# One block for output projection and feed-forward in place of two, with the second token block's difference T2 on VectorE

## The reference, cut to what matters

```python
def swiglu(x, w_gate_up, w_down):
    gate, up = jnp.split(x @ w_gate_up, 2, axis=-1)
    return (jax.nn.silu(gate) * up) @ w_down
...
    for l in range(DEPTH):
        if l < N_A_LAYERS:
            q, k, v, lf = fox_project(rms_norm(h, g_attn[l]), w_a_in[l], b_a_f[l])
            h = h + merge_heads(fox_attention_prompt(q, k, v, lf)) @ w_a_out[l]
        else:
            j = l - N_A_LAYERS
            if j == 0:
                kb_p, vb_p = shared_kv(h, g_kv, w_kv)
            q = split_heads(rms_norm(h, g_attn[l]) @ w_b_q[j])
            h = h + merge_heads(band_attention_prompt(q, kb_p, vb_p, rel_bias[j])) @ w_b_out[j]
        h = h + swiglu(rms_norm(h, g_ffn[l]), w_gate_up[l], w_down[l])
    y_prompt = rms_norm(h, g_final)
```

## Time and profile before

| | |
|---|---|
| median of three runs | 3222.82 us (3222.11 to 3222.87) |
| profiled execution | 3220.69 us, its span 3219.0 us |
| mean granted TensorE clock | 0.959 of full speed |
| busy TensorE | 2958.0 us, 92% |
| busy VectorE | 1535.7 us, 48% |
| busy ScalarE | 1094.9 us, 34% |
| busy Pool | 948.5 us, 29% |

### The profile page before, as it was taken

The page is one execution under the profiler, slowest core; times in us unless marked ns, Lnnn a source line. Parts: engine busy times, 40 slices in busy tenths (PEclk is TensorE's granted clock), DMA queues, the critical chain, the costliest instruction groups (busy, mean ns, idle before and its releaser), DMA issues. The chain is left out here.

```text
span 3219.0 us, 47355 instructions
## 1 busy us (share of the span) xinstructions
PE 2958.0 (92%) x17916; PEld 2666.7 (83%) x17916; DVE 1535.7 (48%) x2790; ACT 1094.9 (34%) x2284; POOL 948.5 (29%) x1174
## 2 busy tenths in 40 slices
PE   8999799978599999899999997997968999998998
PEld 6777688867599999788878886886758999997887
DVE  3223188862755555433332222886645555553333
ACT  4223277721422222221133232776133222222112
POOL 1000288840544545200000001433334544540001
PEclk9999899989799999999999998998978999999999
DMA  4799577654422222432127985886331222215222
GB/s 149 176 219 244 174 259 246 212 159 136 160 63 83 71 73 83 149 112 77 49 79 197 250 203 203 261 267 176 95 105 42 83 66 79 83 49 203 85 74 84
DMA packets 479633, 448.93 MB, mean 139 GB/s; under 512 B 44160, under 2 KB 402592, under 8 KB 475184
## 3 DMA queue, kind: packets, MB, share of 16 engines
q1 hardware_dynamic: 479408, 445.91, 46.3%
HBM read 293.77 MB, written 165.81 MB: 143 GB/s over the span
## 5 line engine op out<-in xcount | busy, mean ns | idle before, releaser
L295 PE MATMUL ffn_bank<-ffn_x,ffn_w 128*128 128x256 f32 (+1 forms) x2464 | 732.0, 297 | 32.5 <-DVE ffn_x L1950 11.0
L296 PE MATMUL ffn_bank<-ffn_x,ffn_w 128*128 128x256 f32 (+1 forms) x2464 | 730.5, 296 | 0.0
L297 PE MATMUL ffn_bank<-ffn_x,ffn_w 128*128 128x256 f32 (+1 forms) x2464 | 729.0, 296 | 0.0
L295 PEld LDWEIGHTS ffn_bank<-ffn_x,ffn_w 128*128 128x128 f32 x2464 | 468.8, 190 | 36.0 <-issue 20.1
L296 PEld LDWEIGHTS ffn_bank<-ffn_x,ffn_w 128*128 128x128 f32 x2464 | 468.8, 190 | 0.0
L297 PEld LDWEIGHTS ffn_bank<-ffn_x,ffn_w 128*128 128x128 f32 x2464 | 467.7, 190 | 0.0
L295 PE MATMUL ffn_bank<-ffn_wd,ffn_hid 128*128 128x512 f32 x792 | 310.7, 392 | 28.7 <-DVE ffn_wd L1994 26.1
L296 PE MATMUL ffn_bank<-ffn_wd,ffn_hid 128*128 128x512 f32 x792 | 310.0, 391 | 0.0
L297 PE MATMUL ffn_bank<-ffn_wd,ffn_hid 128*128 128x512 f32 x792 | 310.0, 391 | 0.0
L2007 DVE TENSOR_TENSOR all_h<-ffn_bank,all_h 128x1024 f32<-128x1024 f32 x72 | 88.1, 1224 | 342.0 <-PE ffn_bank L297 342.0
L295 PEld LDWEIGHTS ffn_bank<-ffn_wd,ffn_hid 128*128 128x128 f32 x792 | 150.0, 189 | 61.2 <-issue 26.5
(11 more groups left out here) (269 smaller groups left out, 6288.2 us busy)
## 6 DMA issues: line engine op xcount, KB each, us to landing
ffn_raw<-in_w_gate_up SPq DMA_DIRECT2D x88, 512.0 KB, 5.5
ffn_draw<-in_w_down SPq DMA_DIRECT2D x44, 512.0 KB, 4.8
fox_ks<-k_split SPq DMA_DIRECT2D x16, 1088.0 KB, 5.1
band_ks<-k_split SPq DMA_DIRECT2D x16, 1088.0 KB, 5.0
hidden<-ffn_s SPq DMA_DIRECT2D x44, 288.0 KB, 2.1
hidden<-ffn_u SPq DMA_DIRECT2D x44, 288.0 KB, 2.3
ffn_hraw<-hidden SPq DMA_DIRECT2D x32, 384.0 KB, 3.6
qkvw_raw<-in_w_a_in SPq DMA_DIRECT2D x5, 2048.0 KB, 9.0
```

Source lines behind the costliest of these rows:

```text
L295: pe.matmul(out, xh, wh, start=first, stop=False)
L296: pe.matmul(out, xh, wl, start=False, stop=False)
L297: return pe.matmul(out, xl, wh, start=False, stop=last)
```

## The change

Output projection and feed-forward become one block, `out_ffn_block`, with no meeting of the engines between them. The diff below is cut: the class `Turned`, the chunks of kind "add" in `dense_block` and the old loops are removed and not shown, nor are ScalarE's parts of the same loops.

- Both 512-column halves of the projection are done for one tile before the next (`project`). The second half of the weights is a load of its own at the block's start. Three buffers take the attention's tiles (`RAW = 3`, four before), and a tile's buffer is free when the tile's projection is done.
- The residual add is one instruction of 1024 columns (`first_residual`). The norm of a tile follows the projection by one tile, the transposes of the first four tiles (`EARLY = 4`) stand between the projection's tiles, and the x factors of block 0 are split there too, in the loop's rounds 6 and 7. Six of the seven w factors of the first feature tile (`ROOM = 6`) are split ahead of the last residual add.
- The last three tiles are normalised in place, in `h`, and so only after their store to DRAM (`kept`). The transposes of the last five tiles follow the first five up products, one behind each.
- T2 of block 1 is formed on VectorE (`second_difference`); T2 of block 0 and both T5 stay on Pool.
- Five buffers for w_down (`DRAW = 5`), filled one feature tile earlier; all six rows of the first group are split in the last feature tile, each after the product that last read its place.
- The spreading of the relative-position bias is issued after the projection's second tile, and waited for at the step to the down products. The set-up loads three gain vectors and not five.

```diff
-    DRAW, HRAW = 4, 3
+    DRAW, HRAW, RAW = 5, 3, 3
...
+    EARLY, ROOM = 4, 6
...
+        def normed(n):
+
+            return xn[:, n % 2, :] if n < ROOM else h[:, TILES[n], :]
...
+                def fetch(n):
+                    if n >= RAW:
+                        sp.wait_ge(out_done, n - RAW + 1)
+                    for u in range(2):
+                        sp.dma_start(att_raw[n % RAW][:, u], att_d[u, :, TILES[n] * P:(TILES[n] + 1) * P].rearrange(
+                            "(c p) n -> p c n", p=P)).then_inc(att_in[n % RAW], 16)
+
+                fetch(0)
+                sp.dma_start(wo_raw[1][:], out_v[:, :, WC:2 * WC]).then_inc(w2_in, 16)
+                for n in range(1, RAW):
...
+                for n in range(NT):
+                    if n + RAW < NT:
+                        fetch(n + RAW)
+                    elif n + RAW < NT + 2:
+                        sp.wait_ge(out_done, n + 1)
+                        load_weights(n + RAW - NT)
+                    sp.wait_ge(res_done, n + 1)
+                    sp.dma_start(h_d[:, TILES[n], :], h[:, TILES[n], :]).then_inc(kept[TILES[n]], 16)
+                    if distances and n == 1:
+                        distances.store(sp)
+                if keep:
+                    keep(sp)
...
+                    if f == FT - 2:
+                        sp.wait_ge(wl_ready, NB * FT)
+                        for n in range(DRAW - 1):
+                            load_down(n)
...
+                        sp.wait_ge(hid0_stored[0], 16 * (FT // 2))
+                        sp.wait_ge(hid1_stored[0], 16 * (FT // 2))
+                        for n in range(DRAW - 1, QF[0]):
+                            load_down(n)
...
+                def sums_spread(n):
...
+                    pool.tensor_copy(rows[:, n % 2], inv[:, TILES[n], :].rearrange("p (u o) -> p u o", o=1)
+                                     .to_broadcast([P, HEADS, HD])).then_inc(rows_ready, 1)
+                    x = att_raw[n % RAW]
+                    pool.wait_ge(att_in[n % RAW], 32 * (n // RAW + 1))
+                    for half_ in range(2):
+                        part = slice(4 * half_, 4 * half_ + 4)
+                        pool.tensor_tensor(out=x[:, 0, part], in0=x[:, 0, part], in1=x[:, 1, part], op=ALU.add
...
+                for n in range(NT):
+                    if n:
+                        rsqrt(TILES[n - 1])
+                    if n + 2 < NT:
+                        sums_spread(n + 2)
+                    if n == EARLY + 1:
+                        differences(0)
...
+                    if q == 0:
+                        act.wait_ge(prod, products(FT - 1, c // 2, 0))
...
+                        squares(TILES[n - 1])
+                    if distances and n == 1:
+                        distances.act(act)
+                    if n == EARLY + 2:
+                        for i in range(4):
+                            x_high(0, i)
+                    if n == EARLY + 3:
+                        for i in range(4, NB):
+                            x_high(0, i)
+                for i in range(ROOM):
...
                 def scaled(t):
                     n = turn_of[t]
                     if n == 0:
                         dve.wait_ge(gain_in, 16)
                     dve.wait_ge(st.rs_ready, n + 1)
-                    if n >= 2:
+                    if n >= ROOM:
+                        dve.wait_ge(kept[t], 16)
+                    elif n >= 2:
...
+                def second_difference():
+
+                    dve.wait_ge(evac_done, evacs[LAST_OF[1]])
+                    dve.wait_ge(diff_done, diffs[LAST_OF[1]])
+                    dve.tensor_tensor(x_in(1, 1), x_in(1, 6), x_in(1, 4), ALU.subtract).then_inc(t_done, 1)
+
...
                 def down_low(n):
                     q, c = feature_of(n)
                     dve.wait_ge(dh_ready, n + 1)
+                    if q == 0:
+                        dve.wait_ge(prod, products(FT - 1, 3 + c // 2, 0))
...
+                att_low(1)
+                for n in range(1, NT):
+                    first_residual(n - 1)
+                    if n < NT - 1:
+                        att_scale(n + 1)
+                        att_low(n + 1)
+                    scaled(TILES[n - 1])
+                    if 2 <= n - 2 < EARLY:
+                        subtract(TILES[n - 2])
+                    if n == EARLY + 2:
+                        for i in range(4):
+                            x_low(0, i)
+                    if n == EARLY + 3:
+                        for i in range(4, NB):
+                            x_low(0, i)
+                for i in range(ROOM):
                     w_low(0, i)
-                    if i == 2:
-                        scaled(TILES[6])
-                events = events_of(0)
-                for x, (p, y) in enumerate(events):
+                first_residual(NT - 1)
+                scaled(TILES[NT - 1])
...
+                    if x == NT - EARLY - 1:
+                        second_difference()
+                        w_low(0, ROOM)
...
+                        if f == FT - 1 and 4 <= x < 4 + QF[0] - 1:
+                            down_low(x - 4)
+                        if f == FT - 1 and x == NB + 2:
                             hid_low(0, 0)
-                for n in range(DRAW, QF[0]):
-                    down_low(n)
+                        if f == FT - 1 and x == NB + 3:
+                            down_low(QF[0] - 1)
...
+                def project(n):
+                    pe.wait_ge(al_ready, 2 * n + 2)
+                    if n >= 2:
+                        pe.wait_ge(res_done, n - 1)
+                    x = att[n % RAW]
+                    for half_ in range(2):
+                        for c in range(KC):
+                            if n == 0:
+                                pe.wait_ge(wol_ready, KC * half_ + c + 1)
+                            last = product(pe, out_slot(n)[:, half_, :], x[:, 1, c, :], x[:, 0, c, :],
+                                           wo_high[half_][:, c, :], wo_low[half_][:, c, :], c == 0, c == KC - 1)
+                    last.then_inc(out_done, 1)
+
...
+                for n in range(NT):
+                    if n + 1 < NT:
+                        spread_sums(n + 1)
+                    if 0 <= n - 2 < EARLY:
+                        turn(TILES[n - 2])
+                    project(n)
                 for x, (p, y) in enumerate(events_of(0)):
-                    if x < 5:
-                        turn(TILES[4 + x])
                     multiply(0, p, y)
+                    if x < NT - EARLY:
+                        turn(TILES[EARLY + x])
```

More of the change, by code:

```diff
@@ L49 @@
 H_AT = 16512
-SPACE_AT = H_AT + 38720
+SPACE_AT = H_AT + 38656
 SPACE = 43264
@@ L196, in ready @@
         pe.wait_ge(self.low_ready, 2 * t + 2)
[L199 to L257, removed]
-            sp.dma_start(self.raw[:, t % self.RAW, u], self.src[u, :, t * P:(t + 1) * P].rearrange("(c p) n -> p c n", p=P)
-                         ).then_inc(self.loaded[t % self.RAW], 16)
-    def high(self, act, t):
-        for half in range(2):
-            part = slice(4 * half, 4 * half + 4)
-            act.wait_ge(self.scaled_done, 2 * t + half + 1)
-            act.activation(self.xh[:, part, t * P:(t + 1) * P], self.raw[:, t % self.RAW, 0, part], ACT.Copy
-                           ).then_inc(self.high_ready, 1)
-    def low(self, dve, t):
-        for half in range(2):
-            part, cols = slice(4 * half, 4 * half + 4), slice(t * P, (t + 1) * P)
-            dve.wait_ge(self.high_ready, 2 * t + half + 1)
-            dve.tensor_tensor(self.xl[:, part, cols], self.raw[:, t % self.RAW, 0, part],
-                              f32(self.xh[:, part, cols]), ALU.subtract).then_inc(self.low_ready, 1)
-    def ready(self, pe, t):
-        pe.wait_ge(self.low_ready, 2 * t + 2)
@@ L336, in chunks_of @@
     def chunks_of(eng, body):
-        before = {k: [0] * len(v) for k, v in dmas_of("add").items()}
+        before = {k: [0] * len(v) for k, v in dmas_of("").items()}
         for n, kind in enumerate(kinds):
@@ L524, in _ @@
                         load_x(sp, 0, 2)
[L525 to L527 removed]
+                    for i in range(PIECES):
                         part = slice(i * KC // PIECES, (i + 1) * KC // PIECES)
@@ L533, in _ @@
                         gates.load(nc, sp)
-                    if turned_src is not None:
-                        for t in range(1, NT):
-                            src.fetch(sp, t)
                     seen = {}
@@ L625, in chunk @@
                                 chunk_high(act, ck.n + 1)
-                            if storing and not (first and t == 0):
+                            if not (first and t == 0):
                                 empty(act, ck, t - 1 if first else t)
@@ L689, in chunk @@
                             multiply(pe, ck.n, t)
-                            if first and storing:
+                            if first:
```

(9 more changed lines are left out.)

399 lines of the change are left out of this document (217 added, 182 removed).

## The result

The changed kernel takes 3149.15 us (median of 4 runs, 3145.47 to 3150.11) against 3222.85, a ratio of 0.9768 (95% interval 0.9752 to 0.9785): 73.7 us faster. Ratios here are estimated over the single runs of both kernels, so they differ a little from the quotient of the medians (0.9771 here). The forecast was 3113, its range 3086 to 3148; the time lies 1 us outside it and 36 us above the forecast. The profiled execution took 3148.24, its span 3146.5, 72.5 shorter than before, at a mean granted clock of 0.974 (0.959 before).

The account below looks back on a forecast made before the run. TensorE bounds the steady work, so only its waits and half-clock stretches give time back: 2 x 42.2 for projection and seam, less 4 for the bias copy, plus 28.3 and 1.3, make 110 off 3222.8: 3113 us, range 3086 to 3148.

Parts of the forecast that it names:

- I remove both waits, 12.9 + 13.2: Steps from up to down products: TensorE's waits for w_down's low part go, 26.1 us of the 28.3 forecast there.
- Late next is the last low part: Down step: VectorE has it after the second half's fourth sum; 1.5 us a layer left for it (0 to 5).
- no wait above 2 us before the first down product: Sign expected in the new profile at the down step: TensorE has no wait above 2 us before that product.
- the down step keeps its wait: Rival: a w_down row still comes after the last product, or its split queues behind sums; 31 back, 3141 us, chance 0.07.
- The bias copy: First layer's projection: the 5 MB copy delays the sixth tile's load, so TensorE stands for 4 us (0 to 8).
- the 15: Projection: the forecast is wrong if residual adds lie more than 15 us apart.
- The steady loop: Gate-and-up loop: TensorE bounds it, its instructions stay, so the change was priced at nothing there.
- its first up product: Seam after the projection: it comes right behind the last projection matmul, moving from 818.68 to 788.3, 30.4 us earlier.
- The first feature tile: Seam: from first up product to that tile's last sum, 59.8 us becomes 48.0; the forecast is wrong at 60.
- the six low parts: First feature tile, second x block, on VectorE: left at 12.80 us; a quiet Pool would make them 9.3.
- its row of 1.55: Earlier trace's row, a 128x1280 subtraction on VectorE: used to price T2 there at 1.55 us and six quiet low parts at 9.3.
- The rival of slower tile loads: Projection: tile loads set the pitch; whole gain gone at a landing of 39 us, about 3257 at 45; chance 0.05.

Follow-up runs that it names:

- 64 bytes: Changed kernel with everything of the joined block 64 bytes higher in SBUF: 3142.13 us; the same shift with two other edits (split order, bias copy): 3097.63 us.
- 128: Changed kernel with everything of the joined block 128 bytes higher in SBUF, no instruction changed: 3139.06 us, ratio 0.9744.
- 32: Changed kernel with the joined block 32 bytes higher in SBUF: 3137.04 us, repeat 3134.31; with split-order and bias-copy edits too: 3098.04, repeat 3095.11.

## Why the prediction was wrong

**The step that failed** is "I remove both waits, 12.9 + 13.2": forecast 28.3 for both steps with all their terms, measured 2.4. The rows of w_down were split in time, as worked out, and the trace has no wait for them. But the sum then asked only for the last of these rows ("Late next is the last low part"), and not what else the second token tile needs. That is a hidden split queued behind row 6, whose load the change left behind nine reloads. The trace of before showed it only as waits of 0.9 and 1.7 us at the second tile, because the older wait had let row 6 come in. The sign that the prediction set itself, no wait above 2 us before the first down product, came true and did not see it: the new waits, 13.9 and 15.1 us, stand behind that product. The rival "the down step keeps its wait" had 0.07 and 3141; it was the outcome, by a mechanism that I had not named. (Its "31 back" is 28.3 in the sum that gives 3141.) This step's 26 us alone would have left the time at some 3139, inside the range; the two that follow took it out.

**The bias copy** cost 12.9 us in TensorE's first projection (124.7 us from its first matmul at 676.08 to the first up product at 800.77, against 111.8 in layer 2, 2218.72 to 2330.51) where 4 were set, with 0 to 8 as bounds. One pair of residual adds lies 23.9 us apart there, past the 15 that the prediction named as a sign of being wrong. The copy starts 3 us before the sixth tile's load is released and not 9: SP waits 6.7 us for the 48 KB line to land (705.64 to 712.33) before it may issue it. The rest was about right: 19.5 us for the copy, 21.12 for issuing the eight small ones; the load lands 27.8 us after its release (715.5 to 743.28) and not 23. It was held in SP's program: it is issued at 734.16, when the copy has landed. So the order within a ring, for which the prediction cites the Trainium skill (DMA: Bandwidth & Descriptors, "Queues, rings and completion order"), was not put to the test by this load.

**The steady loop** was costed at nothing because its instructions stay; it lost 8.4 us. This step had no bound at all, though the prediction named longer steady feature tiles as a sign of being wrong: they went from 22.21 to 22.40.

**What held.** The first projection matmul went at 676.08 (forecast 677.6); the second layer's residual adds lie 12.65 us apart through the middle of the projection (12.8); its first up product comes 0.2 us behind the last projection matmul, 29.6 earlier counted from the reciprocal (30.4). The first feature tile takes 45.2 us in the first layer and 45.0 in the second (48.0 forecast; 59.8 and 61.5 before), 2.1 of the difference because the six low parts take 10.73 and not the 12.80 of the earlier trace rows. Pool is busy for 6.3 us beside them, and for 9.4 before; the rule of the Trainium skill (SBUF — State Buffer, "Who interferes with whom") points the same way. (The section also lets VectorE's two-port modes contend, which the prediction leaves out; it gives a subtraction of two tensors none.) The prediction read its row of 1.55 as having Pool's difference beside its end; by the earlier trace rows that difference runs beside all but the first 0.3 us of it, so 1.55 was no price for a quiet Pool. In the changed kernel a low part that begins beside a quiet Pool takes 1.48. T2 took 1.49 us (1.55), but brought nothing that the median shows. The rival of slower tile loads did not come up: outside the start and the bias copy no tile's load made TensorE wait.

## What to carry to other kernels

When a wait is removed, walk the next two consumers, not one: list for each what it reads, and what stands ahead of that on every engine's program; an operand that is long in SBUF can be late because its split is queued behind something that nobody needs yet. A copy moved beside other work costs at its start (the wait for its own source) as well as in its length. And a loop whose instructions stay may still change when the tiles are laid out anew: compare its matmul rate first.

## What the hardware showed that was not expected

The 128x256 matmuls of the steady loop ran at one of four constant rates, 84 of them in 10.08, 9.97, 9.89 or 9.80 us, at a granted clock of 1.00, with TensorE busy throughout; within a layer the rate held for 20 feature tiles. Unshifted it was 10.07 or 10.08 in all five kernels and both layers (ten of ten), with 64 bytes 9.89 (four of four), with 128 9.96 or 9.97 (two of two), with 32 9.80 in six layers and 9.89 in two, not the same in each execution. The 128x320 matmuls took 12.32 in all. What sets the rate is open; on 42 feature tiles it is worth up to 11.6 us.

VectorE and Pool held each other up in rows that read as if each waited for a whole instruction of the other. In the changed kernel a low part of VectorE that started at 820.02, while Pool's T5 ran (819.59 to 822.89), took 4.21 us and ended 1.3 us behind it, where 1.48 is its time beside a quiet Pool; Pool's next instruction, begun at 822.85, took 2.53 us, and 1.29 at 793.38, where VectorE was idle.
